# Masked blocks for the first level of a triangular inverse: from GpSimd to VectorE

## The chip, the cores and the metric

The kernel runs on one core of one Trainium2 chip. Times are device microseconds (us) of that core from launch to end. The engines are TensorE (PE; PEld are its weight loads), VectorE (DVE), ScalarE (ACT), GpSimd (POOL) and SyncE (SP, which issues most DMAs). Each works through its own instructions in order, and they wait for each other by semaphores.

## The reference

Two transformer-like blocks on 512 tokens of width 1024, in fp32. The part that the change touches is the gated delta rule of the first block (8 heads, 2 directions, chunks of 64 tokens):

```python
lower = jnp.where(tri_strict, jnp.einsum('bhncd,bhnsd->bhncs', k_beta, k) * decay, 0.0)
rhs = jnp.concatenate([v * beta[..., None], k_beta * jnp.exp(g)[..., None]], axis=-1)
sol = lax.linalg.triangular_solve(lower, rhs, left_side=True, lower=True, unit_diagonal=True)
```

Ahead of it stand a norm, the input projection, a gated depthwise convolution over 31 positions with layer norm, and short convolutions on q, k and v. Behind it stand output projections, a gated feed-forward layer and a per-layer gate. The second block has two feed-forward layers and a mixer of pooling and windowed attention.

## The kernel before

Activations lie transposed, 128 channels on the partitions by 512 tokens. Every weight product is made from split operands: w_hi and w_lo, a_hi and a_lo, three matmuls for each (L618). ScalarE makes the high parts (L1163, L1222, L1435), VectorE the low ones (L1725 for weights, L1782 for activations).

The delta stage runs 8 rounds, R = 0 to 7: two halves of four heads, each with four chunks of 128 tokens. A round treats J = 8 problems at once (4 heads, 2 directions), and in a 128x128 problem the two diagonal blocks of 64 are inverted first, in LEVELS = 6 doubling steps. The matrix L of a round is `en`, 128 partitions x 8 x 128. Its diagonal blocks lie at partitions 0 to 63, columns 0 to 63, and at partitions 64 to 127, columns 64 to 127. A level multiplies them by a 0/1 mask from `consts` into `ls`, which has two buffers, used in turn.

The order of work in a round:

- TensorE: rows of decays (L888) and Gram products (L893), then 16 filler matmuls, k by q (L899), and 17 fillers. Fillers are parts of weight products (`gap`, list GAP) that cover the waits of the inverse. Then for level 0 it waits for `ls` and makes c0 from ls[:, 0] (L907, 32 small matmuls, recorded at L872), 4 fillers, and from level 1 on it waits for `ls` and for `ub` (L910), makes y = c0, 4 fillers, then uy and ty from `tb` and `yb`.
- VectorE: et, en (L2010 to L2019), L itself (L2025, signalled as `L`); in round 6 the residual tiles a_lo 6 and 7 of the convolution's output (L2027 to L2029); `gap(R, 0)` and `gap(R, 1)`, which in rounds 0 to 3 hold 2 + 4 taps of the depthwise convolution (L1800, L1803; list TAP); then tb from ls[:, 0] (L2034) and ub from c0 (L2036). After that come w_lo of the next weight unit, taps, and updates of ub (L2041), tb (L2048) at each level.
- ScalarE: exponentials (L1453 to L1457), in round 6 a_hi 6 and 7, then two copies of the diagonal blocks of `en` into the dense tile `lc` (L1462, L1463).
- GpSimd: waits for `lc`, makes levels 0, 1 and 2 (level 2 waits for ub, as it reuses the buffer of level 0), multiplies qd (L2441), then makes levels 3 to 5. Ahead of round 6 it makes a_lo 0 to 5 (L2468).

The taps that remain of the convolution are dealt out over rounds 0 to 3 and are all done by the end of round 3; rounds 4 to 7 have none. `S("ls")` counts the levels, 6 a round.

Of the kernel before, what the change touches and what calls it, by code (L numbers as in the profile page):

```python
# [17 lines left out]
ALU = mybir.AluOpType  # L18
ACT = mybir.ActivationFunctionType

P = 128
# [6 lines left out]
HH = 4  # L28
# [5 lines left out]
W64 = 64  # L34
LEVELS = 6
# [15 lines left out]
C_ID, C_ONE, C_TRI, C_LVL, C_I64 = 0, P, 2 * P, 4 * P, 4 * P + 2 * LEVELS * W64  # L51
# [68 lines left out]
def build(nc, a, out):  # L120

    ctx = ExitStack()
    with ctx:
        sems = {}

        def S(name):
            if name not in sems:
                sems[name] = ctx.enter_context(nc.semaphore(name))
            return sems[name]
# [6 lines left out]
        def at(name, cols, dtype=F32, offset=None, shape=None):  # L136

            if offset is None:
                offset = base[0]
                base[0] += cols * 4 + (-cols * 4) % 32  # L140
            assert offset + cols * 4 <= first + ALL, (name, offset + cols * 4 - first - ALL)
            return nc.alloc_sbuf_tensor_at(name, shape or [P, cols], dtype, offset=offset)
# [10 lines left out]
        consts = at("consts", C_END)  # L153
# [36 lines left out]
        en = at("en", J * P, shape=[P, J, P])  # L190
        et = at("et", J * P, shape=[P, J, P])
        lc = at("lc", J * W64, shape=[P, J, W64])
        ls = at("ls", 2 * J * W64, shape=[P, 2, J, W64])
# [251 lines left out]
        def cslot(t):  # L445

            return cacc[:, t - 1, :] if t in (1, 2) else cpad[:, max(t - 2, 0), 0:T]

        def csum_in(t):

            return oT[:, KT - 2 + (t > 0)] if t in (0, KT - 1) else cslot(t)

        def wait(eng, name, value):

            if not isinstance(value, int) or value > 0:
                eng.wait_ge(S(name), value)

        def ev_wait(eng, key):

            o = O.at[key]  # L460
            eng.wait_ge(S("ev" + O.reader[o]), O.count(o))
# [15 lines left out]
        def quad(ap, n=HH):  # L477

            return ap.rearrange("p (n c) -> p n c", n=n)
# [8 lines left out]
        def chunk(d, r):  # L488

            return r if d == 0 else NC - 1 - r  # L490
# [24 lines left out]
        def set_count(s, t):  # L515
            return SETS.index(s) * KT + t + 1
# [1203 lines left out]
        def _(dve):  # L1720
# [270 lines left out]
            lo_, hi_ = slice(0, W64), slice(W64, P)  # L1991

            def delta(R):
                half, r = divmod(R, NC)

                def scal(k, j):
                    d, hh = divmod(j, HH)
                    q = d * 8 + HH * half + hh
                    return gat[:, k, chunk(d, r), q:q + 1]
# [7 lines left out]
                for d in range(2):  # L2007

                    sl, q = slice(d * HH, d * HH + HH), d * 8 + HH * half
                    ins = dve.tensor_tensor(et[:, sl], pA[:, sl], gat[:, 2, chunk(d, r), q:q + HH].unsqueeze(2)  # L2010
                                            .to_broadcast([P, HH, P]), ALU.subtract)
# [5 lines left out]
                for d in range(2):  # L2017
                    sl = slice(d * HH, d * HH + HH)
                    ins = dve.scalar_tensor_tensor(et[:, sl], et[:, sl], 0.0, past[d].unsqueeze(1).to_broadcast([P, HH, P]),  # L2019
                                                   ALU.min, ALU.add)  # L2020
# [3 lines left out]
                for j in range(J):  # L2024
                    ins = dve.scalar_tensor_tensor(en[:, j], pB[:, j], scal(1, j), en[:, j], ALU.mult, ALU.mult)  # L2025
                ins.then_inc(S("L"), 1)
                if R == 6:  # L2027
                    for t in range(6, KT):
                        low("conv", t, cslot(t))  # L2029
# [7 lines left out]
                for lv in range(1, LEVELS):  # L2037
# [15 lines left out]
                    if lv in (1, 2):  # L2053
# [3 lines left out]
                        s = slice((lv - 1) * HH, lv * HH)  # L2057
                        dve.tensor_tensor(et[:, s], pA[:, s], et[:, s], ALU.mult).then_inc(S("qk"), 1)
                    if lv in (3, 4) and r:
# [4 lines left out]
                        for j in range((lv - 3) * HH, (lv - 2) * HH):  # L2064
                            ins = dve.scalar_tensor_tensor(bv[:, j], pA[:, j], scal(3, j), bv[:, j], ALU.mult, ALU.subtract)
# [11 lines left out]
                for d in range(2):  # L2077
                    c = chunk(d, r)
                    dst = oT[:, HH * half:HH * half + HH, c * P:(c + 1) * P]
                    src = pA[:, d * HH:d * HH + HH]  # L2080
                    if r < NC // 2:
                        ins = dve.tensor_copy(dst, src)
                    else:
                        if d == 0:
                            dve.wait_ge(S("o_acc"), R)
                        ins = dve.tensor_tensor(dst, dst, src, ALU.add)
                ins.then_inc(S("o_acc"), 1)
                if r < NC - 1:
                    dve.wait_ge(S("s"), (NC - 1) * half + r + 1)
                    if r == 0:  # L2090
                        for d in range(2):
                            ins = dve.tensor_copy(st[:, d * HH:d * HH + HH], pC[:, d * HH:d * HH + HH])
                    else:
                        for j in range(J):
                            ins = dve.scalar_tensor_tensor(st[:, j], st[:, j], scal(5, j), pC[:, j],
                                                           ALU.mult, ALU.add)
# [4 lines left out]
            for R in range(4):  # L2101
                delta(R)
# [9 lines left out]
            for R in range(4, 8):  # L2112
                delta(R)
# [298 lines left out]
        @block.gpsimd  # L2412
        def _(pool):
            def adds(nu):

                for t in range(1, NORMS[nu] - 1):
                    pool.wait_ge(S("sq"), SQ[nu] + t + 1)
                    wait(pool, "add", AD[nu] + t - 1)
                    pool.tensor_tensor(acc[:], acc[:], sq[:, t % 2, :], ALU.add).then_inc(S("add"), 1)  # L2419

            def delta(R):
                half, r = divmod(R, NC)

                def level(lv):
                    pool.wait_ge(S("lc"), R + 1)
                    wait(pool, "y", LEVELS * R + lv - 1)
                    if lv == 2:
                        pool.wait_ge(S("u_upd"), LEVELS * R + 1)
                    q = C_LVL + lv * 2 * W64
                    mask = quad(consts[:, q:q + 2 * W64], 2).unsqueeze(2).to_broadcast([P, 2, HH, W64])  # L2430
                    pool.tensor_tensor(ls[:, lv % 2].rearrange("p (d h) c -> p d h c", d=2),  # L2431
                                       lc[:].rearrange("p (d h) c -> p d h c", d=2), mask, ALU.mult)\
                        .then_inc(S("ls"), 1)

                level(0)
                level(1)
                level(2)
                pool.wait_ge(S("eg"), R + 1)
                for d in range(2):
                    s, c = slice(d * HH, d * HH + HH), chunk(d, r)  # L2440
                    ins = pool.tensor_tensor(qd[:, s], qd[:, s], qT[:, :, c * P:(c + 1) * P], ALU.mult)  # L2441
                ins.then_inc(S("qdm"), 1)
                for lv in range(3, LEVELS):
                    level(lv)

            pool.wait_ge(S("in_s"), 32)
            adds(1)

            for R in range(4):
                if R == 0:  # L2450
                    pool.wait_ge(S("g_all"), 1)
                    pool.wait_ge(S("trc"), 2 * HH)
                delta(R)
            pool.wait_ge(S("tap"), len(TAPS))
            for t in range(1, KT):
                wait(pool, "csum", t - 1)
                pool.tensor_tensor(acc[:], csum_in(0) if t == 1 else acc[:], csum_in(t), ALU.add)\
                    .then_inc(S("csum"), 1)
            for t in range(1, KT):
                pool.wait_ge(S("cvs"), t + 1)  # L2460
                wait(pool, "cva", t - 1)
                pool.tensor_tensor(rstd[:], rstd[:], tmps[t % 2][:], ALU.add).then_inc(S("cva"), 1)
            for R in range(4, 8):
                if R == 6:
                    for t in range(6):
                        pool.wait_ge(S("a_hi"), set_count("conv", t))
                        pool.wait_ge(S("a_lo"), set_count("conv", t) - 1)
                        pool.tensor_tensor(a_lo[:, t], cslot(t), a_hi[:, t].bitcast(F32), ALU.subtract)\  # L2468
                            .then_inc(S("a_lo"), 1)
                delta(R)  # L2470
            def full_adds(p):

                for t in range(1, FULL[p]):
                    pool.wait_ge(S("hq"), HQ[p] + t + 1)
                    wait(pool, "add", HA[p] + t - 1)
                    pool.tensor_tensor(acc[:], acc[:], sq[:, t % 2, :], ALU.add).then_inc(S("add"), 1)  # L2476

            for nu in (2, 3):
                adds(nu)
            for p in range(2):  # L2480
                full_adds(p)
            pool.wait_ge(S("zero"), 4)
            for g in reversed(range(PT_)):

                ev_wait(pool, ("mu", g))
                wait(pool, "wd", PT_ - 1 - g)
                for q in range(g + 1):
                    src = up[:, g] if q == 0 else win[:, (q - 1) % 2]
                    ins = pool.tensor_tensor(win[:, q % 2, PW:], src[:, PW:], src[:, PW - (1 << q):PW + T - (1 << q)],
                                             ALU.add)  # L2490
                    if q < g:
                        n_add = sum(range(g + 1, PT_)) + q + 1
                        ins.then_inc(S("wadd"), 1)
                        pool.wait_ge(S("wadd"), n_add)
                ins.then_inc(S("win"), 1)
            for nu in (6, 7):
                adds(nu)
            for p in (2, 3):
                full_adds(p)
# [73 lines left out]
```

## Time and profile before

| what | value |
|---|---|
| median of 3 runs | 2299.31 us (2299.02 to 2302.66) |
| the profiled execution | 2300.46 us, of it 2298.6 us span |
| mean granted TensorE clock | 0.973 |
| busy: PE, DVE, ACT, POOL | 2205.4, 1282.0, 826.8, 203.2 us |
| ls on GpSimd (L2431), 48 blocks | 77.0 us, 1.61 us each in the mean |

An engine's idle time counts only where another one, or the end, waits for what it does next; which this is, the chain of work that ended last tells.

### The profile page before, as it was taken

How to read it: one execution, taken by the hardware profiler on the slowest of the kernel's cores; microseconds unless marked ns; L12 is line 12 of the kernel's file. 1: busy time of each engine (PE TensorE's matmuls, PEld its weight loads, DVE VectorE, ACT ScalarE, POOL GpSimd, SP SyncE). 2: the span in 40 equal slices, each digit the busy share in tenths (PEclk: the TensorE clock that was granted, in tenths of full speed). 3: DMA queues.
4: the chain of work that ended last, by engine and by line, in shares of the span. 5: the costliest groups of instructions: out<-in, count | busy, mean ns of one | idle time of the engine just before them, and what ended most of it. 6: DMA issues, size and time to landing. Idle time of an engine off the chain costs nothing.

```text
span 2298.6 us, 34911 instructions
## 1 busy us (share of the span) xinstructions
PE 2205.4 (96%) x14254; PEld 1840.2 (80%) x14254; DVE 1282.0 (56%) x1899; ACT 826.8 (36%) x1273; POOL 203.2 (9%) x142
## 2 busy tenths in 40 slices
PE   7998999998999999999999999999999899999998
PEld 5877777777788878888888888888888579888887
DVE  4687899987555555444443454444227835444413
ACT  4345433335444233332322352322224544232322
POOL 0100222211213101000000100000000210000000
PEclk9999999999999989999999989999999989999999
DMA  4242111112111124333332312333222112323331
GB/s 156 76 135 67 43 45 55 56 58 68 33 47 55 58 83 149 105 100 93 102 113 85 119 56 92 100 95 117 88 75 73 37 55 65 94 97 98 109 101 50
DMA packets 56202, 189.88 MB, mean 83 GB/s; under 512 B 6288, under 2 KB 8720, under 8 KB 56080
## 3 DMA queue, kind: packets, MB, share of 16 engines
q1 hardware_dynamic: 53200, 182.88, 24.8%
q10 hardware_dynamic: 2880, 5.24, 0.6%
q8 instruction: 92, 1.51, 0.3%
q14 instruction: 30, 0.25, 0.0%
HBM read 178.66 MB, written 9.44 MB: 82 GB/s over the span
## 4 chain that ended last, share of the span: by engine, by line
PE 81%; DVE 11%; issue 5%; ACT 2%; DMA 1%; POOL 0%; SPq 0%; DVEq 0%; ACTq 0%; POOLq 0%
PE pg L618 69%; PE pC L872 3%; DVE oT L1803 2%; DVE w_lo L1725 1%; PE pB L649 1%; DVE sacc L1917 1%; DVE cpad L1803 1%; PE pB L872 1%; PE pC L656 1%; ACT w_hi L1163 1%; PE pA L696 1%; DVE cacc L1803 1%; DMA w_raw<-in_w_in 0%; PE pB L656 0%; PE pB L680 0%
## 5 line engine op out<-in xcount | busy, mean ns | idle before, releaser
L618 PE MATMUL pg<-a_hi,w_hi 128*128 128x512 f32 (+1 forms) x1984 | 778.7, 392 | 16.3 <-DVE a_lo L1782 4.8
L618 PE MATMUL pg<-a_hi,w_lo 128*128 128x512 f32 (+1 forms) x1984 | 769.4, 388 | 0.0
L618 PE MATMUL pg<-a_lo,w_hi 128*128 128x512 f32 (+1 forms) x1984 | 768.7, 387 | 0.0
L1725 DVE TENSOR_TENSOR w_lo<-w_raw,w_hi 128x1024 fp32r<-128x1024 f32 (+3 forms) x299 | 387.0, 1294 | 408.3 <-ACT w_hi L1163 406.9
L1163 ACT ACTIVATE w_hi<-w_raw 128x1024 fp32r<-128x1024 f32 (+3 forms) x299 | 329.6, 1102 | 632.3 <-PE pg L618 622.5
L618 PEld LDWEIGHTS pg<-a_hi,w_hi 128*128 128x128 f32 x1984 | 379.7, 191 | 95.9 <-issue 9.8
L618 PEld LDWEIGHTS pg<-a_hi,w_lo 128*128 128x128 f32 x1984 | 379.0, 191 | 72.8 <-issue 1.2
L618 PEld LDWEIGHTS pg<-a_lo,w_hi 128*128 128x128 f32 x1984 | 379.9, 191 | 70.3 <-issue 0.7
L618 PE MATMUL pg<-h_hi,w_hi 128*128 128x512 f32 (+1 forms) x572 | 215.7, 377 | 0.6 <-DVE w_lo L1725 0.6
L618 PE MATMUL pg<-h_hi,w_lo 128*128 128x512 f32 (+1 forms) x572 | 214.5, 375 | 0.0
L618 PE MATMUL pg<-h_lo,w_hi 128*128 128x512 f32 (+1 forms) x572 | 212.4, 371 | 0.0
L2177 DVE TENSOR_TENSOR tmp<-pg,rstd 128x512 f32<-128x512 f32 x66 | 45.6, 691 | 188.6 <-PE pg L618 188.6
L618 PEld LDWEIGHTS pg<-h_hi,w_lo 128*128 128x128 f32 x572 | 107.3, 188 | 21.3
L618 PEld LDWEIGHTS pg<-h_lo,w_hi 128*128 128x128 f32 x572 | 107.4, 188 | 20.4
L618 PEld LDWEIGHTS pg<-h_hi,w_hi 128*128 128x128 f32 x572 | 107.5, 188 | 19.2 <-DVE w_lo L1725 1.0
L2431 POOL TENSOR_TENSOR ls<-lc,consts 128x512 f32<-128x512 f32 x48 | 77.0, 1610 | 458.9 <-ACT lc L1463 402.4
L2476 POOL TENSOR_TENSOR acc<-acc,sq 128x512 f32<-128x512 f32 x22 | 29.7, 1351 | 818.2 <-ACT sq L1206 818.2
L1803 DVE SCALAR_TENSOR_TENSOR cpad<-cpad,vec 128x512 f32<-128x512 f32 x120 | 91.0, 821 | 0.2
L1534 ACT ACTIVATE h_hi<-tmp 128x512 f32 (+1 forms) x66 | 41.7, 632 | 131.7 <-DVE tmp L2181 131.7
L2419 POOL TENSOR_TENSOR acc<-acc,sq 128x512 f32<-128x512 f32 x22 | 33.0, 1500 | 553.2 <-ACT sq L1180 552.9
L1917 DVE SCALAR_TENSOR_TENSOR sacc<-pad,swt,sacc 128x512 f32<-128x512 f32 x96 | 76.5, 797 | 3.4
L2186 DVE TENSOR_TENSOR h_lo<-tmp,h_hi 128x512 f32 (+1 forms) x66 | 45.7, 693 | 58.3 <-ACT h_hi L1534 58.3
(353 smaller groups left out, 2321.0 us busy)
## 6 DMA issues: line engine op xcount, KB each, us to landing
w_raw<-in_w_gu SPq DMA_DIRECT2D x132, 512.0 KB, 3.5
w_raw<-in_w_in SPq DMA_DIRECT2D x74, 512.0 KB, 3.6
w_raw<-in_w_dn SPq DMA_DIRECT2D x48, 704.0 KB, 4.1
spill_g<-tmp ACTq DMA_DIRECT2D x16, 256.0 KB, 2.0
w_raw<-in_w_co SPq DMA_DIRECT2D x8, 512.0 KB, 3.7
w_raw<-in_w_do SPq DMA_DIRECT2D x8, 512.0 KB, 4.1
w_raw<-in_w_wo SPq DMA_DIRECT2D x8, 512.0 KB, 4.0
w_raw<-in_w_pg SPq DMA_DIRECT2D x8, 512.0 KB, 4.3
```

The source lines that it names most:

```text
L618: ins = pe.matmul(dst[:, cols], w_of(w, n % 2, k), b(k)[:, cols], start=first and q == 0, stop=last and q == len(todo) - 1)
L872: ins = pe.matmul(dst[s, j, :], lhs[s, j, :], id64[s, :] if rhs is None else rhs[s, j, :], start=True, stop=True)
L1163: act.activation(w_hi[:, n % 2, 0:c], w_raw[:, n % 4, 0:c], ACT.Copy).then_inc(S("w_hi"), 1)
L1534: act.activation(h_hi[:, m] if isinstance(i, int) else h_hi[:, bass.ds(m, 1)].rearrange("p a n -> p (a n)"), tmp2[:], ACT.Copy).then_inc(S ...
L1725: dve.tensor_tensor(w_lo[:, n % 2, 0:c], w_raw[:, n % 4, 0:c], w_hi[:, n % 2, 0:c].bitcast(F32), ALU.subtract).then_inc(S("w_lo"), 1)
L1803: ins = dve.scalar_tensor_tensor(y, src, w, y, ALU.mult, ALU.add)
L1917: ins = dve.scalar_tensor_tensor(y, src, w, y, ALU.mult, ALU.add)
L2177: dve.tensor_tensor(tmp2[:], bu, rstd[:], ALU.mult).then_inc(S("evD"), 1)
L2186: dve.tensor_tensor(at_m(h_lo), tmp2[:], at_m(h_hi).bitcast(F32), ALU.subtract)\
L2419: pool.tensor_tensor(acc[:], acc[:], sq[:, t % 2, :], ALU.add).then_inc(S("add"), 1)
L2431: pool.tensor_tensor(ls[:, lv % 2].rearrange("p (d h) c -> p d h c", d=2), lc[:].rearrange("p (d h) c -> p d h c", d=2), mask, ALU.mult)\
L2476: pool.tensor_tensor(acc[:], acc[:], sq[:, t % 2, :], ALU.add).then_inc(S("add"), 1)
```

## The change

VectorE makes the two products for level 0 itself. It waits for its own `L`, multiplies each diagonal half of `en` by the mask into ls[:, 0], and signals `ls`, all of it ahead of round 6's residuals and of the taps. GpSimd drops level 0; its level 1 now also waits until VectorE has signalled level 0, so that the count stays in order. ScalarE still copies both halves into `lc` for the other levels.

```diff
@@ VectorE, delta(R), behind L @@
                     ins = dve.scalar_tensor_tensor(en[:, j], pB[:, j], scal(1, j), en[:, j], ALU.mult, ALU.mult)
                 ins.then_inc(S("L"), 1)
+                dve.wait_ge(S("L"), R + 1)
+                mask = quad(consts[:, C_LVL:C_LVL + 2 * W64], 2).unsqueeze(2).to_broadcast([P, 2, HH, W64])
+                for s in (lo_, hi_):
+                    ins = dve.tensor_tensor(ls[s, 0].rearrange("p (d h) c -> p d h c", d=2),
+                                            en[s, :, s].rearrange("p (d h) c -> p d h c", d=2), mask[s], ALU.mult)
+                ins.then_inc(S("ls"), 1)
                 if R == 6:
@@ GpSimd, delta(R) @@
                 def level(lv):
                     pool.wait_ge(S("lc"), R + 1)
+                    if lv == 1:
+                        pool.wait_ge(S("ls"), LEVELS * R + 1)
                     wait(pool, "y", LEVELS * R + lv - 1)
...
-                level(0)
                 level(1)
                 level(2)
```

## Rows read from the trace of the kernel before

**Rows 1.** The page: the chain that ended last, by engine

```profile
PE 81%; DVE 11%; issue 5%; ACT 2%; DMA 1%; POOL 0%; SPq 0%; DVEq 0%; ACTq 0%; POOLq 0%
```

**Rows 2.** Busy us by engine in three stretches, then PEclk, DMA share, GB/s

```profile
298.00:364.00 66.00, 61.79 (x763) 51.13 (x761) 61.86 (x103) 22.66 (x40) 14.08 (x8) 0.97 0.14 49
...
718.50:722.00 3.50, 3.45 (x15) 2.73 (x15) 1.99 (x2) 1.75 (x3) 2.55 (x2) 1.00 0.02 5
...
308.60:312.30 3.70, 3.68 (x36) 2.73 (x36) 3.63 (x4) 0.00 (x0) 2.22 (x2) 0.54 0.18 71
```

**Rows 3.** The chain in order of time, rounds 2 and 3: start, us, what

```profile
382.42 3.58 DVE cpad L1803 x3
...
482.93 0.75 DVE oT L1803
```

**Rows 4.** Timeline of VectorE and TensorE, round 4: start, us, what, [idle before]

```profile
606.64 1.76 DVE L2034 TENSOR_TENSOR tb<-consts,ls 128x512 f32<-128x512 f32 x1 [2.70 <-POOL ls L2431]
...
609.31 1.15 PE L872 MATMUL pC<-consts,ls 64*64 64x64 f32 x32
```

**Rows 5.** Timeline of round 6: VectorE, TensorE, GpSimd

```profile
717.82 1.27 DVE L1782 TENSOR_TENSOR a_lo<-cpad,a_hi 128x512 fp32r<-128x512 f32 x2
...
718.55 0.50 PE L618 MATMUL pg<-a_hi,w_hi 128*128 128x512 f32 x1 [1.07 <-DVE a_lo L1782]
...
719.28 2.55 POOL L2431 TENSOR_TENSOR ls<-lc,consts 128x512 f32<-128x512 f32 x2 [4.60 <-ACT lc L1463]
```

**Rows 6.** The chain in order of time, behind that restart

```profile
718.55 3.73 PE pg L618 x15
```

**Rows 7.** Timeline of GpSimd, round 1

```profile
304.86 4.93 POOL L2431 TENSOR_TENSOR ls<-lc,consts 128x512 f32<-128x512 f32 x2 [42.87 <-ACT lc L1463]
```

**Rows 8.** Timeline of VectorE, round 1: L, taps, tb, ub, ub of level 1

```profile
301.31 2.16 DVE L2025 SCALAR_TENSOR_TENSOR en<-pB,gat,en 128x128 f32<-128x128 f32 x8
303.39 4.06 DVE L1803 SCALAR_TENSOR_TENSOR cpad<-cpad,vec 128x512 f32<-128x512 f32 x6
308.60 1.75 DVE L2034 TENSOR_TENSOR tb<-consts,ls 128x512 f32<-128x512 f32 x1 [1.15 <-POOL ls L2431]
310.42 0.69 DVE L2036 TENSOR_TENSOR ub<-consts,pC 128x512 f32<-128x512 f32 x1
...
315.69 0.69 DVE L2041 TENSOR_TENSOR ub<-ub,pC 128x512 f32<-128x512 f32 x1 [1.78 <-PE pC L872]
```

**Rows 9.** Timeline of VectorE, rounds 2 and 3

```profile
374.31 1.74 DVE L2034 TENSOR_TENSOR tb<-consts,ls 128x512 f32<-128x512 f32 x1 [1.16 <-POOL ls L2431]
375.97 0.68 DVE L2036 TENSOR_TENSOR ub<-consts,pC 128x512 f32<-128x512 f32 x1
...
380.19 0.69 DVE L2041 TENSOR_TENSOR ub<-ub,pC 128x512 f32<-128x512 f32 x1 [0.72 <-PE pC L872]
...
433.55 6.13 DVE L1803 SCALAR_TENSOR_TENSOR oT<-cpad,vec,oT 128x512 f32<-128x512 f32 x6
```

**Rows 10.** Groups by shape on VectorE, rounds 0 to 3: busy, mean ns | idle before

```profile
L2045 DVE TENSOR_TENSOR en<-ub,pC 64x512 f32<-64x512 f32 x4 | 2.8, 692 | 0.1
...
L2044 DVE TENSOR_TENSOR en<-ub,pC 64x512 f32<-64x512 f32 x4 | 2.7, 672 | 0.4 <-PE pC L872 0.4
```

**Rows 11.** Timeline of TensorE: level 1 of round 0, level 0 of round 1

```profile
248.55 1.15 PE L872 MATMUL pC<-ub,ls 64*64 64x64 f32 x32
...
308.62 1.76 PE L872 MATMUL pC<-consts,ls 64*64 64x64 f32 x32 [2.39 <-POOL ls L2431]
```

**Rows 12.** Timeline of VectorE: taps and ub of round 0, taps of round 1

```profile
242.14 1.98 DVE L1800 TENSOR_SCALAR cpad<-cpad,vec 128x512 f32<-128x512 f32 x2
244.04 2.44 DVE L1803 SCALAR_TENSOR_TENSOR cpad<-cpad,vec 128x512 f32<-128x512 f32 x2
...
247.54 0.69 DVE L2036 TENSOR_TENSOR ub<-consts,pC 128x512 f32<-128x512 f32 x1 [0.46 <-PE pC L872]
...
332.27 0.99 DVE L1800 TENSOR_SCALAR cpad<-cpad,vec 128x512 f32<-128x512 f32 x2
```

## The prediction

> **What bounds the kernel.** I read the chain that ended last first: TensorE has 81% of it, VectorE 11%, GpSimd rounds to 0% [rows 1]. So the change can only act where TensorE or VectorE is at its limit inside the eight rounds of the delta stage (about 232 to 826 us), and each round has to be asked separately. Two regimes are to be seen. In rounds 0 to 3 VectorE also works off the convolution's taps: in round 1 it is busy 61.86 of 66 us, and in rounds 2 and 3 the chain in order of time is a nearly unbroken run of VectorE pieces from 382.42 us to the end of the taps; the first and last of its 20 tap pieces are shown [rows 2, 3]. What delays VectorE there delays the end. In rounds 4 to 7 there are no taps. In round 4 VectorE sits idle 2.70 us for the first masked block, but TensorE, still in its filler matmuls, takes that block at 609.31 us with no wait [rows 4]; rounds 5 and 7 look the same. Round 6 differs: VectorE also makes two residual tiles (a_lo 6 and 7) right behind L, and TensorE has stopped 1.07 us for them. From its restart at 718.55 us the chain is TensorE's nearly without a break; the first piece of that run is shown [rows 5, 6].
>
> Then the timelines of VectorE, GpSimd and TensorE around L. In round 1 GpSimd starts its two blocks at 304.86 us, in the middle of six taps. Level 0 is not ready before 308.6, although an undisturbed block is half of 2.55 us, 1.27 (round 6) [rows 5, 7]. The taps run on unhindered (4.06 us for six, 0.68 each) and VectorE then idles 1.15 us. Its tb, fed only from SBUF, takes 1.75 us beside GpSimd's level 1 where the ub behind it takes 0.69: a stall of 1.07 [rows 8]. In round 3 it goes the other way: the same six taps take 6.13 us, 2.07 more, and nothing is waited for afterwards [rows 9]. So the two engines take turns, and one GpSimd block costs VectorE about 1.07 us whoever goes first.
>
> **What the change costs on VectorE.** Added per round: a wait for L and two products on 64 partitions x 512. Nearest rows: two 64x512 tensor_tensor in a row, 0.672 and 0.692 us, on alternate partition halves as here [rows 10]. They read PSUM, the masks read SBUF; I take 0.69 each. The taps used to start 0.08 us before L's last record ended (303.39 against 301.31 + 2.16) [rows 8]; waiting for L loses that and some 0.06 more, and a step between instructions 0.04. Together 2 x 0.69 + 0.18 = 1.56 us a round. If the two overlapped like neighbouring taps (0.08 each) it is 1.4; if TensorE's or ScalarE's reads slowed them it is not seen in any row.
>
> The Trainium skill bears on the 0.69: "VectorE: DVE Perf Modes", section on two Vector instructions with no wait between them, says that an instruction whose inputs start in another partition quadrant than the last one's is held until that one is finished. The two products start on partitions 0 and 64, and by that rule they do not overlap (1.56); without it the price is 1.4. The row of 0.692 behind 0.672 agrees.
>
> **What it gives back, round by round.** T is the end of ub, from which TensorE's level 1 starts. GpSimd keeps one block (level 1) in this stretch, so one stall c stays: 1.07 if it lands on a tap or tb, 0.6 if it slips behind tb and level 1 itself is late, 0 if it fits beside ub, which reads PSUM.
> Round 1: gone are the idle 1.15 and one stall of 1.07, together 2.22. T moves by 1.56 - 2.22 + c = -0.66 to +0.41. On top, T is not the whole of it before: ub of level 1 starts 4.58 us behind T (315.69 - 311.11), in round 2 only 3.54 (380.19 - 376.65) [rows 8, 9]. The 1.04 more is TensorE, which was late with c0 after its wait of 2.39 us and ran at clock 0.54 [rows 2, 11]. After, c0 goes at once, but TensorE then stands from about 308.6 to T, 2.2 to 2.7 us, so the clock may fall again, one block later. I take half of 1.04: round 1 = -0.3 us, bounds -1.7 and +0.4.
> Round 2: the same 2.22 (1.16 idle, 1.06 stall) [rows 9], without the 1.04: +0.2, bounds -0.7 and +0.4.
> Round 3: gives back one stall pair, 2.07: 1.56 - 2.07 + 1.07 = +0.5; I take +0.3, bounds -0.5 and +0.6.
> Round 0: taps stalled by 2.0 (1.98 for two tensor_scalar that take 0.99 in round 1, and 2.44 for two that take 1.41) [rows 12]. 1.56 - 2.0 + 1.07 = +0.6, but ub idled 0.46 for TensorE's c0 and ended (247.54 + 0.69 = 248.23) 0.3 before TensorE wanted it at 248.55 [rows 11, 12]. Hidden: 0. Without that cover it would be 0.6.
> Rounds 4, 5, 7: 1.56 us of masks replace 2.7 us of idleness [rows 4]: 0. If the 2.7 were not there, it would be 1.56 each.
> Behind the masks queue also w_lo of the next filler unit (not due before c0) and, in round 6, a_lo 6 and 7.
> Round 6: a_lo starts at 717.82 before, now 1.56 later, and TensorE's restart at 718.55 with it: +1.5 [rows 5]. Then GpSimd: its level 1 becomes free at about 719.3, exactly when a_lo begins, where before it began (719.28) after a_lo was done. If it goes first or between the two, up to 1.07 more. I take +2.0, bounds 1.5 and 2.6, with the clock still full: it was full in the 3.5 us behind the present pause of 1.07 [rows 2]. The pause grows to 2.6, and 2.39 in round 1 was enough for a fall; one such stretch costs 3.70 x (1 - 0.54) = 1.7 us. That is the dear end, +4.3.
> GpSimd's own 8 x 1.27 us less is worth nothing in itself. ScalarE's lc copies stay and run beside the masks; level 1 waits for both, and both end within 0.2 us of each other.
>
> **Sum.** 0 - 0.3 + 0.2 + 0.3 + 2.0 = +2.2 us. The profiled execution took 2300.46 us (span 2298.6 and 1.86 around it), so 2302.7; the median of the runs lies 1.15 lower: 2301.5. No change that can be measured: 0.2% of this time is 4.6 us, about what runs can tell here.
>
> **Rivals.**
> *A, the forecast* (+0.5 to +3.5 us, 2299.8 to 2302.8): 0.55.
> *B, slower: round 6.* One mechanism: the residuals pushed behind the masks lengthen TensorE's stop so that its clock falls. Place 717.5 to 724 us. Price 1.5 + 1.1 + 1.7 = 4.3, with the +0.2 of rounds 1 to 3 and their spread some 5: 2304.3. For it: 2.6 us is more than the 2.39 that sufficed. Against: a stop of 1.07 did not, and the fall depends on how the stop lies. It decides once the clock falls and GpSimd gets in as well. 0.15.
> *C, a small gain: the waits in rounds 1 to 3 are worth more.* c is near 0 and TensorE's clock stays up in round 1: -1.7 - 0.7 - 0.5 + 1.5 = -1.4: 2297.9. For it: TensorE really waited 2.39 us for GpSimd in round 1. Against: every round shows the turn-taking. 0.22, of which 0.05 past -4.6, if falls of the clock elsewhere vanish too. The Trainium skill, "GPSIMD Engine Reference", section 4.1, sends elementwise products to VectorE, as GpSimd is about 2 times slower. In this trace a whole block is 1.27 us there, but here the diagonal halves need two VectorE products, 1.38. Had that rule's factor held (0.64 a block), the sum would by this estimate be some 3.7 us lower (0.92 less in each of rounds 1, 2, 3 and 6).
> *D, no effect anywhere:* the masks hide in round 6 too, because something else sets the restart there. Against: the wait names a_lo. About -0.1 to +0.3: 2299.4. 0.08.
> From these: faster by over 0.2% 0.05, within 0.2% 0.80, slower 0.15. The range takes in C and B: 2297.4 to 2305.0.
>
> **What the next profile would show.** Right: two VectorE products of 0.68 to 0.70 us on 64x512 in each round; ls on GpSimd 40 instead of 48; TensorE's wait of 2.39 us for ls in round 1 gone and a wait for ub in its place; tb directly behind the taps; the restart in round 6 2.2 to 3.3 us behind the end of L, where it was 0.66; rounds 4, 5, 7 as long as before. Wrong: masks above 0.8 us, taps more stalled than before, TensorE waiting for level 1 in round 1, a pause longer than 3.7 us in round 6, or falls of the clock at places that the change doesn't touch.

## The result and the profile after

| | before | after |
|---|---|---|
| median of 17 runs each | 2299.31 us | 2304.12 us |
| lowest to highest | 2295.77 to 2302.66 | 2300.03 to 2306.9 |
| profiled execution, its span | 2300.46, 2298.6 | 2304.26, 2302.4 |
| mean granted TensorE clock | 0.973 | 0.971 |

The ratio is 1.002, with a 95% interval of 1.0013 to 1.0026: the change costs 4.8 us between the medians, 3.0 to 6.0 us by the interval. That lies inside the forecast range (2297.4 to 2305.0), 2.6 us above the predicted time and right at the bound of 0.2% that separates "no change" from "slower". It lies outside the narrower span of the forecast itself, rival A's 2299.8 to 2302.8. A second comparison later on, `change_again` below, gave 1.0021. Two executions in the later comparisons fell in a far slower state (3030 and 4358 us) and are left out of every median and ratio.

The page of the changed kernel: the chain by engine, and the masked blocks of GpSimd.

```profile
PE 80%; DVE 15%; ACT 2%; issue 2%; DMA 1%; SPq 0%; DVEq 0%; ACTq 0%
...
L2439 POOL TENSOR_TENSOR ls<-lc,consts 128x512 f32<-128x512 f32 x40 | 66.6, 1665 | 476.5 <-DVE ls L2030 369.8
```

GpSimd makes 40 blocks where it made 48. VectorE's share of the chain has grown from 11 to 15% against [rows 1], but this reading says nothing on the change: two of the three control runs below, which are the kernel before unedited, show 15% as well.

VectorE in round 1 of the changed kernel, then TensorE, then GpSimd: start, us, what, [idle before].

```profile
302.92 2.16 DVE L2025 SCALAR_TENSOR_TENSOR en<-pB,gat,en 128x128 f32<-128x128 f32 x8
305.12 1.39 DVE L2030 TENSOR_TENSOR ls<-en,consts 64x512 f32<-64x512 f32 x2
306.54 5.11 DVE L1803 SCALAR_TENSOR_TENSOR cpad<-cpad,vec 128x512 f32<-128x512 f32 x6
311.56 0.68 DVE L2040 TENSOR_TENSOR tb<-consts,ls 128x512 f32<-128x512 f32 x1
312.17 0.67 DVE L2042 TENSOR_TENSOR ub<-consts,pC 128x512 f32<-128x512 f32 x1
...
308.81 1.15 PE L872 MATMUL pC<-consts,ls 64*64 64x64 f32 x32
...
312.99 1.15 PE L872 MATMUL pC<-ub,ls 64*64 64x64 f32 x32 [1.91 <-DVE ub L2042]
...
306.64 1.81 POOL L2439 TENSOR_TENSOR ls<-lc,consts 128x512 f32<-128x512 f32 x1 [43.04 <-DVE ls L2030]
```

Read beside [rows 8]: the masks stand as one piece of 1.39 us behind L, the six taps take 5.11 us instead of 4.06 because GpSimd's level 1 falls into them (a stall of 1.05), and tb follows with no idle time and undisturbed, 0.68 instead of 1.15 idle and 1.75. TensorE's wait of 2.39 us for `ls` [rows 11] is gone. In its place it waits 1.91 us for ub.

Round 6: VectorE, TensorE, GpSimd.

```profile
718.01 2.15 DVE L2025 SCALAR_TENSOR_TENSOR en<-pB,gat,en 128x128 f32<-128x128 f32 x8
720.19 1.39 DVE L2030 TENSOR_TENSOR ls<-en,consts 64x512 f32<-64x512 f32 x2
721.61 2.38 DVE L1782 TENSOR_TENSOR a_lo<-cpad,a_hi 128x512 fp32r<-128x512 f32 x2
...
719.34 0.40 PE L618 MATMUL pg<-a_hi,w_lo 128*128 128x512 f32 x1
722.36 0.79 PE L618 MATMUL pg<-a_hi,w_hi 128*128 128x512 f32 x1 [2.62 <-DVE a_lo L1782]
722.95 0.63 PE L618 MATMUL pg<-a_lo,w_hi 128*128 128x512 f32 x1
723.38 0.63 PE L618 MATMUL pg<-a_hi,w_lo 128*128 128x512 f32 x1
...
721.71 1.73 POOL L2439 TENSOR_TENSOR ls<-lc,consts 128x512 f32<-128x512 f32 x1 [4.78 <-ACT lc L1463]
```

Four stretches of the changed kernel, columns as in [rows 2]: round 1 behind c0, round 1 behind the stop of 1.91 us, round 6 behind the restart, all of round 6.

```profile
308.80:312.30 3.50, 2.28 (x37) 1.68 (x36) 3.50 (x7) 1.12 (x2) 0.00 (x0) 1.00 0.19 75
312.90:316.40 3.50, 3.41 (x76) 2.92 (x78) 2.79 (x3) 2.23 (x7) 3.39 (x2) 1.00 0.35 90
722.00:725.40 3.40, 3.00 (x6) 1.99 (x7) 2.59 (x3) 0.00 (x0) 1.44 (x1) 0.53 0.02 5
711.00:768.00 57.00, 54.34 (x711) 44.49 (x711) 31.88 (x58) 19.39 (x37) 15.61 (x11) 0.97 0.17 55
```

TensorE's stop has grown from 1.07 [rows 5] to 2.62 us, and the clock behind it is 0.53 where it was 1.00 [rows 2]: matmuls of 0.63 us instead of 0.40. In round 1 it is the other way: 0.54 behind the stop of 2.39 us before, 1.00 behind the stop of 1.91 us now.

The table puts the start of each round (the first et on VectorE) in the changed kernel against the kernel before, in us, each from its profiled execution.

| | round 0 | 1 | 2 | 3 | 4 | 5 | 6 | 7 | end |
|---|---|---|---|---|---|---|---|---|---|
| lag of its start | 0.98 | 1.62 | 0.66 | 0.96 | 2.25 | 2.25 | 2.27 | 5.52 | 3.79 |
| start of L to ub of level 1, before | 13.22 | 14.38 | 13.18 | 12.94 | 13.14 | 11.43 | 12.07 | 11.17 | |
| the same, after | 13.85 | 13.47 | 13.46 | 13.46 | 13.14 | 11.45 | 15.33 | 11.18 | |

Round 6 stands out with +3.26, and the lag grows by 3.25 over it. The 0.98 of round 0 arises ahead of every changed instruction. Over rounds 3 to 4 the lag grows by 1.29, of which 0.52 is the stretch behind L; beside the other 0.77 stands a stretch of low clock at 585 us that is 10.2 us long and was 6.8. The unedited kernel shows the longer stretch and +0.81 in the control `only_r6`, so it need not be the change's.

### The profile page after: what moved, and what is told of

It reads as the page before. It is cut to its first block, busy times and chain, and to the rows that moved or that the text cites. A ratio compares the mean times of both kernels' runs of the same rounds, so it can differ in the third digit from the quotient of the medians.

```text
span 2302.4 us, 34913 instructions
## 1 busy us (share of the span) xinstructions
PE 2207.9 (96%) x14254; PEld 1843.3 (80%) x14254; DVE 1286.8 (56%) x1915; ACT 827.0 (36%) x1273; POOL 193.5 (8%) x134
## 4 chain that ended last, share of the span: by engine, by line
PE 80%; DVE 15%; ACT 2%; issue 2%; DMA 1%; SPq 0%; DVEq 0%; ACTq 0%
PE pg L618 68%; DVE cpad L1803 3%; PE pC L872 3%; DVE w_lo L1725 2%; DVE oT L1803 2%; DVE sacc L1917 1%; PE pB L649 1%; PE pB L872 1%; PE pC L656 1%; ACT w_hi L1163 1%; PE pA L696 1%; DVE cacc L1803 1%; DMA w_raw<-in_w_in 0%; PE pB L656 0%; DVE a_lo L1782 0%
## 5 line engine op out<-in xcount | busy, mean ns | idle before, releaser
L2439 POOL TENSOR_TENSOR ls<-lc,consts 128x512 f32<-128x512 f32 x40 | 66.6, 1665 | 476.5 <-DVE ls L2030 369.8
```

## The experiments

Medians and ratios are to runs of the kernel before on the same chip, whose medians were 2300.1 to 2301.0 us. A ratio is the record's estimate with its 95% interval, and can differ by up to 0.0005 from the quotient of the two medians. The profiles of one and the same program differ by up to 2.8 us in span (see the controls), while the length of round 6 (its start to the start of round 7) repeats within 0.1 us: 58.59 to 58.67 us in four profiles of the kernel before, 61.89 in both of the changed one. So round 6 is judged by that length, and the rounds with taps by the time from L to ub of level 1.

**resid_first.** The masks stay on VectorE everywhere, but in round 6 behind the residuals.

```diff
+                if R == 6:
+                    for t in range(6, KT):
+                        low("conv", t, cslot(t))
                 dve.wait_ge(S("L"), R + 1)
...
-                if R == 6:
-                    for t in range(6, KT):
-                        low("conv", t, cslot(t))
                 gap(R, 0)
```

> All rounds on VectorE, but in round 6 the two residual tiles are made ahead of the masks. Theory R: TensorE's restart in round 6 comes 0.66 us behind the end of L, as in the kernel before, after a pause of 1.07 us and at full clock; in all -0.5 to +1.5 us to the kernel before. Rival V: +3 to +6 us, as the changed kernel.

2300.82 us, ratio 1.0003 (0.9994 to 1.0012). Round 6 takes 58.65 us. Its timeline, VectorE and TensorE:

```profile
721.68 1.27 DVE L1782 TENSOR_TENSOR a_lo<-cpad,a_hi 128x512 fp32r<-128x512 f32 x2
722.88 1.38 DVE L2033 TENSOR_TENSOR ls<-en,consts 64x512 f32<-64x512 f32 x2
...
722.41 0.50 PE L618 MATMUL pg<-a_hi,w_hi 128*128 128x512 f32 x1 [1.07 <-DVE a_lo L1782]
722.74 0.40 PE L618 MATMUL pg<-a_lo,w_hi 128*128 128x512 f32 x1
```

The stop is 1.07 us again, the clock full, and the loss gone, though the 16 level-0 products of the eight rounds are still all VectorE's. The order in round 6 is what costs, not the work.

**between.** The masks between residual tiles 6 and 7 of round 6.

```diff
+                if R == 6:
+                    low("conv", 6, cslot(6))
                 dve.wait_ge(S("L"), R + 1)
...
                 if R == 6:
-                    for t in range(6, KT):
-                        low("conv", t, cslot(t))
+                    low("conv", 7, cslot(7))
```

> In round 6 the masks stand between residual tiles 6 and 7. The same delay of 1.5 us as in the changed kernel, but cut in two pauses of TensorE, one of 1.07 us ahead of tile 6 and one of about 1.5 us ahead of tile 7. If the clock falls because of one long pause (theory R), it stays up here and the round costs +1.5 us instead of +3.2. If any pauses of this sum bring it down, +3.2 us. Rival V: no difference to the changed kernel in the whole time.

2303.16 us, ratio 1.0009 (1.0 to 1.0018). Round 6 takes 59.99 us, +1.35. TensorE in it:

```profile
720.19 0.50 PE L618 MATMUL pg<-a_hi,w_hi 128*128 128x512 f32 x1 [1.07 <-DVE a_lo L1782]
...
722.22 0.50 PE L618 MATMUL pg<-a_hi,w_hi 128*128 128x512 f32 x1 [1.06 <-DVE a_lo L1782]
722.56 0.40 PE L618 MATMUL pg<-a_lo,w_hi 128*128 128x512 f32 x1
```

```profile
722.20:725.60 3.40, 3.38 (x25) 2.57 (x26) 1.65 (x1) 1.06 (x1) 1.10 (x1) 1.00 0.02 5
```

Two stops of 1.07 and 1.06 us, and the clock stays full. Here 1.06 us more of stopping cost 1.35; in the changed kernel 1.55 more (2.62 less 1.07) cost 3.25. The 1.7 beyond the stop itself appear only with the single long one, and that is the price that the prediction worked out for one stretch of low clock.

**only_r6b.** VectorE makes level 0 in round 6 alone; in the others GpSimd does, as before.

```diff
+DVE_ROUNDS = (6,)
...
-                dve.wait_ge(S("L"), R + 1)
+                if R in DVE_ROUNDS:
+                    dve.wait_ge(S("L"), R + 1)
...
-                    if lv == 1:
+                    if lv == 1 and R in DVE_ROUNDS:
...
+                if R not in DVE_ROUNDS:
+                    level(0)
                 level(1)
```

> The change in round 6 alone (GpSimd makes level 0 in the other seven rounds, as before). Theory R: 3.2 us more between the starts of rounds 6 and 7 if the clock falls (restart 1.5 us later and one slow stretch worth 1.7), 1.5 if it doesn't, and +1.5 to +4 us in all. If the loss of the changed kernel sat elsewhere, nothing to be seen here beyond the 2 us by which a kernel without any change was off in its profile.

2302.31 us, ratio 1.0005 (0.9997 to 1.0014). Round 6 takes 61.93 us, +3.29, and the picture is that of the whole change, 1.65 us later; TensorE:

```profile
724.01 0.79 PE L619 MATMUL pg<-a_hi,w_hi 128*128 128x512 f32 x1 [2.62 <-DVE a_lo L1783]
724.60 0.63 PE L619 MATMUL pg<-a_lo,w_hi 128*128 128x512 f32 x1
```

The 3.3 us of round 6 need nothing of the other rounds. In the timed runs the part is worth 1.5 us between the medians, and its interval ends at 3.2, just short of the 3.3 of the profile.

**only_r03b.** The same edit with `DVE_ROUNDS = (0, 1, 2, 3)`.

> The change in rounds 0 to 3 alone. From the start of L to ub of level 1: round 1 -0.9 us (0 if the clock falls in the new pause), round 2 +0.3, round 3 +0.5; in all within 1.5 us of the kernel before. If VectorE's 1.46 us a round counted in full, +4 to +6 us.

2300.26 us, ratio 1.0001 (0.9992 to 1.001). L to ub: 13.21, 14.93, 13.46, 13.47 us, against before -0.01, +0.55, +0.28, +0.53; round 6 58.62. Rounds 0, 2 and 3 came as predicted. Round 1 differs from the changed kernel, which gained 0.91 there. TensorE in it, and the stretch behind:

```profile
305.78 1.15 PE L873 MATMUL pC<-consts,ls 64*64 64x64 f32 x32
...
310.97 1.29 PE L873 MATMUL pC<-ub,ls 64*64 64x64 f32 x32 [2.92 <-DVE ub L2044]
```

```profile
311.40:314.80 3.40, 3.40 (x41) 2.44 (x37) 2.24 (x2) 2.50 (x8) 3.40 (x3) 0.56 0.51 151
```

With the same VectorE work c0 starts earlier (4.85 us behind the start of L instead of 5.89), its four fillers are used up earlier, and TensorE then stands 2.92 us for ub; the clock falls to 0.56. In the changed kernel TensorE had come to c0 late, after a stretch of low clock from 292 us that was 6.8 us long instead of 3.4, stood only 1.91 us, and kept its clock. That is worth 1.46 us in one round. What makes that earlier stretch long or short isn't shown: it was long in both profiles of the changed kernel, and short in all four of the versions with the same rounds 0 to 3 (the table at the end of this section).

**extra_r03.** The changed kernel with two more pairs of such products in rounds 0 to 3, written to `tb`, which is overwritten afterwards: VectorE's added work three times over.

```diff
+                if R in EXTRA:
+                    for n in range(2):
+                        for s in (lo_, hi_):
+                            ins = dve.tensor_tensor(tb[s].rearrange("p (d h) c -> p d h c", d=2),
+                                                    en[s, :, s].rearrange("p (d h) c -> p d h c", d=2), mask[s], ALU.mult)
+                        ins.then_inc(S("xtra"), 1)
+                        dve.wait_ge(S("xtra"), 2 * EXTRA.index(R) + n + 1)
```

> The change with two more pairs of 64x512 products on VectorE in rounds 0 to 3, written to a tile that is overwritten later: 2.8 us more of VectorE work behind L in each of these rounds. If VectorE sets the end of rounds 1 to 3 (my theory and rival V alike), each grows by 2.7 to 3.0 us and round 0 by 2.3 to 3.0, 11 us in all on top of the changed kernel. If TensorE's own work sets these rounds, under 3 us.

2320.01 us, ratio 1.0088 (1.0075 to 1.0102). VectorE in round 1:

```profile
311.18 3.80 DVE L2037 TENSOR_TENSOR tb<-en,consts 64x512 f32<-64x512 f32 x4
315.01 4.06 DVE L1804 SCALAR_TENSOR_TENSOR cpad<-cpad,vec 128x512 f32<-128x512 f32 x6
```

The four products take 3.80 us, since GpSimd's level 1 now stalls them and the taps run free (4.06): net 2.75 more a round, 11.0 in all. L to ub grew by 17.9 us over the four rounds (17.37, 18.26, 17.72, 18.78). The low-clock stretches of the whole program sum to 145 us, against 135 after. VectorE's time there is on the path, as the prediction had it. But I expected 11 us in all, and the runs show some 15 to 16 us over the changed kernel: a microsecond of delay cost more than a microsecond, some 1.6 from L to ub. Where the excess goes was not tested; the longer stretches of low clock are one candidate.

**from_lc.** VectorE makes level 0 from the dense `lc` by one product on 128 partitions, behind the first two taps and, in round 6, behind the residuals.

```diff
                 gap(R, 0)
+                dve.wait_ge(S("lc"), R + 1)
+                mask = quad(consts[:, C_LVL:C_LVL + 2 * W64], 2).unsqueeze(2).to_broadcast([P, 2, HH, W64])
+                dve.tensor_tensor(ls[:, 0].rearrange("p (d h) c -> p d h c", d=2),
+                                  lc[:].rearrange("p (d h) c -> p d h c", d=2), mask, ALU.mult).then_inc(S("ls"), 1)
                 gap(R, 1)
```

> VectorE makes level 0 with one product of 128x512 from the dense copy lc, behind the first two taps (in round 6 behind the residual tiles). The cost per round falls from 1.46 us to 0.6 or 0.7, no wait for lc shows in rounds 0 to 3 (two taps take 1.33 us, the copies 1.3). Expected per round against the changed kernel: -0.8 us in rounds 1, 2, 3, and -3.2 in round 6; against the kernel before -1.0 to -2.5 us in all. If the price of the masks doesn't matter, only the -3.2 of round 6.

2301.01 us, ratio 0.9999 (0.999 to 1.0008). VectorE in round 1:

```profile
306.78 0.69 DVE L2033 TENSOR_TENSOR ls<-lc,consts 128x512 f32<-128x512 f32 x1
307.39 3.75 DVE L1803 SCALAR_TENSOR_TENSOR cpad<-cpad,vec 128x512 f32<-128x512 f32 x4
```

The whole block costs VectorE 0.69, half of the two diagonal products. L to ub is 12.62 and 12.63 us in rounds 2 and 3, 0.56 and 0.31 less than before, and 14.15 and 14.09 us in rounds 0 and 1, +0.93 and -0.29 against before. Round 6 takes 58.62 us. The version undoes the loss. Of what I expected, rounds 2, 3 and 6 came (-0.84, -0.83 and -3.27 against the changed kernel), round 1 did not (+0.62, since it lacks the changed kernel's full clock there), and the gain of 1.0 to 2.5 us on the kernel before is not to be seen.

**extra_r457.** The same extra products in rounds 4, 5 and 7 (`EXTRA = (4, 5, 7)`), to find the size of the cover there.

> The same extra products in rounds 4, 5 and 7. VectorE has 4.4 us of idleness there between tb and the c0 that it waits for, so my theory expects no change at all of these rounds against the changed kernel (under 0.3 us). If it were no cover, +8 us.

2305.92 us, ratio 1.0025 (1.0015 to 1.0034). L to ub: 13.14 in round 4 (+0.00), 12.29 in round 5 (+0.84), 12.29 in round 7 (+1.11). VectorE in round 5:

```profile
661.87 1.39 DVE L2031 TENSOR_TENSOR ls<-en,consts 64x512 f32<-64x512 f32 x2
663.29 3.81 DVE L2037 TENSOR_TENSOR tb<-en,consts 64x512 f32<-64x512 f32 x4
667.13 0.69 DVE L2048 TENSOR_TENSOR tb<-consts,ls 128x512 f32<-128x512 f32 x1
667.74 0.68 DVE L2050 TENSOR_TENSOR ub<-consts,pC 128x512 f32<-128x512 f32 x1
```

No idle time is left ahead of ub: the 3.8 us have used up the cover, which in rounds 5 and 7 is 3.0 and 2.7 us beyond the change's own masks. My expectation took round 4's cover for all three: in the changed kernel VectorE idles 4.41 us ahead of ub in round 4, but only 2.72 and 2.44 in rounds 5 and 7.

Round 6, which this edit leaves alone, takes 62.77 us, 0.88 more than in the changed kernel. TensorE in it, and the stretch behind 724.9 us:

```profile
722.79 0.51 PE L619 MATMUL pg<-a_hi,w_hi 128*128 128x512 f32 x1 [2.61 <-DVE a_lo L1783]
...
724.48 0.51 PE L619 MATMUL pg<-a_hi,w_hi 128*128 128x512 f32 x1 [0.72 <-DVE a_lo L1783]
...
725.36 0.63 PE L619 MATMUL pg<-a_hi,w_hi 128*128 128x512 f32 x1
```

```profile
724.90:728.30 3.40, 3.40 (x10) 2.61 (x9) 0.12 (x1) 1.06 (x1) 0.00 (x0) 0.54 0.02 5
```

The stop is the same 2.61 us, but here the clock is still full at the restart and falls 2.1 us later. So TensorE comes to the second residual tile in time to wait 0.72 us for it, and the low stretch then lies on 3.4 us of unbroken matmuls.

**all_levels.** The kernel before, but in rounds 0 to 3 VectorE makes all six levels from `lc`, 24 products, and GpSimd keeps only qd.

```diff
+                def masked(*levels):
+                    if R >= NC:
+                        return
+                    for lv in levels:
...
+                        dve.tensor_tensor(ls[:, lv % 2].rearrange("p (d h) c -> p d h c", d=2),
+                                          lc[:].rearrange("p (d h) c -> p d h c", d=2), m, ALU.mult)\
+                            .then_inc(S("ls"), 1)
```

> The kernel before, but in rounds 0 to 3 VectorE makes all six levels, each with one 128x512 product from lc; GpSimd keeps qd and all of rounds 4 to 7. If the turn-taking is real (each GpSimd block costs VectorE 1.05 us in these rounds, its own product 0.61), VectorE gains 0.4 us a level and the idle 1.15 of rounds 1 and 2: -2 to -3.5 us a round in rounds 1 to 3, -6 to -10 us in all. If the stalls are no more than a record of overlapping, VectorE's work grows by 6 x 0.61 = 3.7 us a round: +8 to +14 us.

2299.16 us, ratio 0.9997 (0.9988 to 1.0006). Groups by shape on VectorE, 232 to 490 us, and below them all engines in that stretch:

```profile
L1803 DVE SCALAR_TENSOR_TENSOR cpad<-cpad,vec 128x512 f32<-128x512 f32 x120 | 82.1, 745 | 0.2
...
L2007 DVE TENSOR_TENSOR ls<-lc,consts 128x512 f32<-128x512 f32 x24 | 16.2, 687 | 0.2
L2029 DVE SCALAR_TENSOR_TENSOR et<-et,consts 128x512 f32<-128x512 f32 x8 | 9.5, 1231 | 0.1
```

```profile
232.00:490.00 258.00, 232.53 (x2990) 193.76 (x2988) 243.24 (x410) 89.44 (x154) 12.57 (x8) 1.00 0.15 50
```

The same two views of the kernel before:

```profile
L1803 DVE SCALAR_TENSOR_TENSOR cpad<-cpad,vec 128x512 f32<-128x512 f32 x120 | 91.0, 821 | 0.2
```

```profile
232.00:490.00 258.00, 238.31 (x2980) 198.56 (x2978) 243.72 (x385) 89.47 (x154) 53.70 (x32) 0.97 0.15 50
```

The taps shrink from 821 to 745 ns each, 8.9 us of busy time on the 120 of this group alone, yet VectorE is as busy as before (243.24 against 243.72): 24 products of 0.687 cost the 16 us that the stalls of 24 blocks had cost, less some stall that has moved to et. Its products take 1231 ns each where they took 688 before, for they now run beside GpSimd's qd (in round 1 two of them 2.37 us from 299.74 us on, qd 3.16 us from 300.11). The clock is full throughout the stretch, and the starts of rounds 1 to 7 lead by 0.2 to 1.1 us. My expectation of a gain of 6 to 10 us and its rival of a loss of 8 to 14 both fell: break-even.

**r6_gpsimd, only_r6 and only_r03.** These were meant to be the change without round 6, in round 6 alone, and in rounds 0 to 3 alone. My edit chose the rounds by a list named `VEC`, a name that the kernel gives to another list further down, so that no round matched, and all three ran the kernel before unchanged (48 blocks on GpSimd in each). The text on record for each speaks of what was meant.

> The change in all rounds but 6, where GpSimd makes level 0 as before. Theory R (the loss sits in round 6: the residual tiles start 1.5 us later and TensorE's clock falls): the restart of round 6 loses its 3.2 us, and from the start of round 6 to that of round 7 no time is added to the kernel before; the whole kernel stands -0.5 to +1.5 us to the kernel before. Rival V (the loss is VectorE's extra work in rounds 0 to 3, some 1.5 us each): still +3 to +6 us.

> The change in round 6 alone. Theory R: +3.2 us in the stretch from round 6 to round 7 (1.5 of it delay, 1.7 the slower clock), the same as in the changed kernel, and +2.5 to +4 us in all, unless the clock happens not to fall, then +1.5. Rival V: +1.5 us at most in that stretch and within 1 us of the kernel before in all.

> The change in rounds 0 to 3 alone. My theory: round 1 -0.9, round 2 +0.3, round 3 +0.5 us, measured from the end of L to ub of level 1, round 0 within 0.2 unless the clock differs; in all -0.5 to +1 us to the kernel before. Rival V: +3 to +6 us, the whole of the changed kernel's loss.

As tests of the parts they are void; only_r6b and only_r03b replace two of them. They are controls: ratios 1.0004 (0.9994 to 1.0013), 1.0000 (0.9991 to 1.0009), 0.9998 (0.9989 to 1.0006), spans 2300.3, 2301.4 and 2300.7 us where the profile of before has 2298.6, and a round 6 of 58.59, 58.60 and 58.67 us. L to ub in round 0 reads 13.21, 14.11 and 13.21 in them: the +0.63 of the changed kernel in round 0 needs no change.

**change_again.** The changed kernel, unedited.

> The changed kernel once more, unedited, in the same setting as the versions that hold parts of it. The profiles' terms say +3.1 us over the kernel before (round 6 +3.25, rounds 1 to 3 together -0.1), so a ratio near 1.0014; the first comparison gave 1.002 (1.0013 to 1.0026), and the two parts run apart gave 1.0005 and 1.0001. If the two parts act independently and 1.0005 is right for round 6: 1.0006. If they act together: 1.0015 to 1.002. Round 6 to round 7 should again take 61.9 us where the kernel before takes 58.6, in either case.

2304.42 us, ratio 1.0021 (1.0012 to 1.0031), round 6 61.89 us. The 4 to 5 us are the change's, not one comparison's luck. The two parts run apart give 1.0006 together; with intervals of about 0.0009 each the difference of 0.0015 is as large as its own uncertainty (0.0016).

**All profiles together.** Five profiles have the old rounds 0 to 3 (before, the three controls, only_r6b), and six have the change's (after, change_again, resid_first, between, only_r03b, extra_r457). From the start of L to ub of level 1, in us:

| | old | the change's |
|---|---|---|
| round 0 | 13.21 to 14.11 | 13.20 to 14.02 |
| round 1 | 14.26 to 14.42 | 13.47 in two, 14.87 to 14.96 in four |
| round 2 | 13.18 in two, 12.94 or 12.95 in three | 13.46 or 13.47 |
| round 3 | 12.94 to 12.96, once 14.45 | 13.45 to 13.47 |
| start of round 0 to start of round 4 | 362.93 to 365.01, mean 364.06 | 364.30 to 365.14, mean 364.69 |

So the gain of round 1 is the exception and a loss of some 0.5 us the rule, and all that the change does to rounds 0 to 3, +0.6 us between the means, is smaller than the spread of one program.

## Why the prediction came out as it did

**The masks, 1.56 us a round: right.** 1.39 us for the two (8 at a mean of 687 ns in rounds 0 to 3), and with the wait for L and the steps the taps start 3.62 us behind L's start where they started 2.08 behind [rows 8]: 1.54. The held second product, which the Trainium skill states in "VectorE: DVE Perf Modes", section on two Vector instructions with no wait between them, agrees with the trace: 1.39 for two, where two 128x512 subtractions without that change of partitions take 1.27 [rows 5].

**Round 0, nothing: right.** -0.01 in only_r03b; the changed kernel's +0.63 lies inside what a control shows too (+0.89).

**Round 1, -0.3 within -1.7 and +0.4: right in the changed kernel's profiles, by luck.** It is -0.91 there and +0.49 to +0.58 in the four other profiles with the same rounds 0 to 3, beyond the bound. The term's c was 1.05 us, on the taps, as supposed, and T moved by +0.12 after L. That is 0.25 less than 1.54 - 2.22 + 1.05, mostly since tb and ub now each start before the record ahead of them ends. What was left open, whether the clock falls a block later, was indeed open. Where it stays full, ub of level 1 starts 3.55 us behind T, as in round 2, and the whole 1.04 comes back. Where it falls it starts 5.04 us behind T (only_r03b), 0.46 more than before, and the bound of +0.4 had no room for that.

**Rounds 2 and 3, +0.2 and +0.3: right against the profile of before.** +0.28 and +0.52, the same in all six profiles within 0.02. Against three other profiles of the old round 2 its term is +0.52 as well, just beyond the bound of +0.4.

**Rounds 4, 5, 7, nothing: right.** 0.00, +0.02, +0.01; and extra_r457 shows the cover that hid them.

**Round 6, +2.0 "with the clock still full": the term that was too small.** The restart came 2.20 us behind the end of L, as forecast (2.2 to 3.3). GpSimd's block did fall on the residuals, 2.38 us for the two instead of 1.27, but TensorE restarted on the first, so its stop grew by 1.55 only. The clock, however, fell (0.53), and from the restart to c0 it took 5.36 us instead of 3.65 before: 1.7 more, together 3.25 in place of 2.0. That the late second tile cost nothing is itself the slow clock's doing, for the matmuls ahead of it took until it was ready; in extra_r457, where the clock was full for the first 2.1 us, TensorE waited 0.72 us for it. From these rows I estimate 1.55 + 0.72 = 2.3 us for a clock that stays full, inside the 1.5 to 2.6 of the forecast. So the delay and the stall were sized rightly, and the clock was what I had wrong. That is rival B's mechanism and its 1.7, with GpSimd's 1.1 hidden behind the slower matmuls. I had put it at 0.15 although [rows 11] with [rows 2] showed a fall behind 2.39 us and this stop was worked out as 2.6; the row spoke for B more strongly than the chance said.

**The sum.** The terms measured on the rounds of the two profiles are 0 - 0.9 + 0.3 + 0.5 + 3.25 = +3.1 us, where +2.2 was forecast, and rival A's span (+0.5 to +3.5) holds it. The medians say +4.8 and +4.3, outside A's span and nearer B's 2304.3. The missing 1 to 2 us have no place in these two profiles: outside the changed rounds the lag moves both ways (+0.98 ahead of round 0, -1.73 behind round 7) with the place of low-clock stretches that the controls show moving as well. If round 1 goes in most runs as in the four other profiles of the same rounds, the sum is +4.6 and all is explained, and a round 6 as in extra_r457 would add 0.9. Both profiles of the changed kernel show -0.91 and 3.25, so this is only argued and stays open. That the median fell inside the range is owed to B, which the range took in.

**The signs.** Of the signs of being wrong two showed. The clock fell for longer at 220 us, which the change doesn't touch, but a control shows that too. And the taps were stalled more than before, 5.11 us against 4.06 for the six in round 1 and 841 ns against 821 in the mean of 120 (rounds 0 to 3). That sign was badly chosen, since the forecast itself allowed GpSimd's one block to land on a tap.

**Rival C** had its clock in round 1 (1.00, in two profiles of six) but not the rest. **Rival D** is out: the restart in round 6 moved with a_lo, and the round grew by 3.25. "GPSIMD Engine Reference" of the Trainium skill, section 4.1, holds VectorE for some 2 times faster on elementwise products. Measured here: 1.39 us for the block as two diagonal halves against 1.27 for an undisturbed one on GpSimd [rows 5], and 0.69 when it is made from the dense copy (from_lc). So the rule holds for the same shape, and the change gave its gain away by the shape.

## What to carry to other kernels

Before an instruction is put ahead of others in an engine's order, look at every round for what stands right behind it and who waits for that: seven rounds bore these 1.4 us for some 0.6 us or less, the eighth passed them on to TensorE whole, and putting the residuals first took the cost away. Where TensorE's stop would grow to a length that has already dropped the clock somewhere in the same trace, price the fall into the forecast and not only into a rival. And compare a change's profile with a second profile of the unchanged program: chain shares and round starts moved by as much as many an effect.

## What the runs showed of the hardware that was not expected

- TensorE's clock stayed full behind stops of 1.07 and 1.91 us and behind two of 1.07 and 1.06 us with 2 us between their restarts. It was 0.51 (only_r6b) to 0.56 behind stops of 2.39, 2.62 and 2.92 us. Behind one of 2.61 us (extra_r457) it was full for 2.1 us more and then 0.54. One fall cost 1.5 to 1.9 us beyond the stops. In the changed kernel's two profiles a longer stretch of low clock earlier in round 1 went with a shorter stop later, since TensorE came late to its wait (1.91 instead of 2.92 us).
- A GpSimd block (128x512, undisturbed 1.27 us) costs VectorE 1.0 to 1.1 us when it falls on taps (5.11 against 4.06), residuals (2.38 against 1.27) or masks (3.80 for four against twice 1.39), and it is itself held to 1.7 or 1.8 us. VectorE doing the same block alone takes 0.69. Moving all of them in rounds 0 to 3 gained no time, only GpSimd's.
- Executions of one program differ in where its stretches of low clock lie: at 220 us such a stretch is 6.8 us long in three profiles of the kernel before and 17.1 in the fourth.
